# Sums of squares before a normalisation: six of eight tiles are added on VectorE, and TensorE multiplies ones with that sum and with the last two tiles

## The reference

```python
def rms_norm(x, gain):
    xf = x.astype(jnp.float32)
    y = xf * lax.rsqrt(jnp.mean(xf * xf, axis=-1, keepdims=True) + EPS)
    return (y * gain.astype(jnp.float32)).astype(x.dtype)

def swiglu(x, w_in, w_out):
    gate, up = jnp.split(x @ w_in, 2, axis=-1)
    return (jax.nn.silu(gate) * up) @ w_out

    for l in range(DEPTH):
        ...
        hn = rms_norm(h, g_ffn1[l]) * (1.0 + sc1) + sh1
        h = h + 0.5 * (1.0 + gt1) * swiglu(hn, w_ffn1_in[l], w_ffn1_out[l])
        hn = rms_norm(h, g_mix[l]) * (1.0 + sc2) + sh2
        proj = hn @ w_mix_in[l]
        ...
        h = h + (1.0 + gt2) * mixed
        hn = rms_norm(h, g_ffn2[l]) * (1.0 + sc3) + sh3
        h = h + 0.5 * (1.0 + gt3) * swiglu(hn, w_ffn2_in[l], w_ffn2_out[l])
```

## Time and profile before

| | |
|---|---|
| time, median of three runs | 3076.71 us (3075.94 to 3076.88) |
| span of the profiled execution | 3077.4 us |
| TensorE busy in it | 2896.3 us, 94% |
| VectorE busy | 1608.6 us, 52% |
| ScalarE busy | 980.8 us, 32% |
| GpSimd busy | 197.4 us, 6% |

### The profile page before, as it was taken

The page is one execution under the profiler, slowest core; times in us unless marked ns, Lnnn a source line. Parts: engine busy times, 40 slices in busy tenths (PEclk is TensorE's granted clock), DMA queues, the critical chain, the costliest instruction groups (busy, mean ns, idle before and its releaser), DMA issues.

```text
span 3077.4 us, 43060 instructions
## 1 busy us (share of the span) xinstructions
PE 2896.3 (94%) x17732; PEld 2329.1 (76%) x17732; DVE 1608.6 (52%) x2074; ACT 980.8 (32%) x1461; POOL 197.4 (6%) x270
## 2 busy tenths in 40 slices
PE   6999999988999998999999888999989999968996
PEld 5888877676788887888776767888767778658775
DVE  6676575763767524333357744333364446655533
ACT  2222223522322223222334323222324444422322
POOL 2000000230000000000001400000010000013000
PEclk8999999988999999999999889999999999969998
DMA  6556442102456322232211012232221121100231
GB/s 243 196 201 209 153 147 83 58 3 82 162 172 233 115 84 82 88 110 87 98 69 59 16 44 80 87 106 93 84 96 67 64 69 62 58 1 4 72 103 41
DMA packets 45368, 298.62 MB, mean 97 GB/s; under 512 B 5664, under 2 KB 5792, under 8 KB 16800
## 3 DMA queue, kind: packets, MB, share of 16 engines
q1 hardware_dynamic: 36000, 229.31, 22.0%
q0 software_dynamic: 9216, 67.11, 6.4%
HBM read 294.30 MB, written 2.10 MB: 96 GB/s over the span
## 4 chain that ended last, share of the span: by engine, by line
PE 86%; DVE 10%; ACT 2%; issue 1%; DMA 0%; POOL 0%; SPq 0%; DVEq 0%; ACTq 0%; POOLq 0%
PE ps L914 17%; PE ps L915 17%; PE ps L916 17%; PE ps L1181 5%; PE ps L1183 5%; PE ps L1182 5%; PE ps L821 1%; PE ps L1489 1%; PE ps L1490 1%; PE ps L1491 1%; PE ps L2019 1%; PE ps L2003 1%; PE ps L784 1%; PE ps L2016 1%; PE ps L1267 1%; DVE w_lo L891 1%
## 5 line engine op out<-in xcount | busy, mean ns | idle before, releaser
L914 PE MATMUL ps<-hn_hi,w_hi 128*128 128x512 f32 x1536 | 606.5, 395 | 33.9 <-DVE hn_lo L865 23.1
L915 PE MATMUL ps<-hn_lo,w_hi 128*128 128x512 f32 x1536 | 602.3, 392 | 0.0
L916 PE MATMUL ps<-hn_hi,w_lo 128*128 128x512 f32 x1536 | 601.4, 392 | 0.0
L891 DVE TENSOR_TENSOR w_lo<-w_raw,w_hi 128x2048 fp32r<-128x2048 f32 (+3 forms) x229 | 472.4, 2063 | 162.6 <-ACT w_hi L884 162.4
L884 ACT ACTIVATE w_hi<-w_raw 128x2048 fp32r<-128x2048 f32 (+3 forms) x229 | 394.4, 1722 | 115.6 <-PE ps L1183 98.0
L914 PEld LDWEIGHTS ps<-hn_hi,w_hi 128*128 128x128 f32 x1536 | 291.4, 190 | 100.4 <-issue 39.5
L1181 PE MATMUL ps<-hn_hi,w_hi 128*128 128x512 f32 x776 | 326.0, 420 | 20.4 <-DVE hn_lo L865 13.0
L915 PEld LDWEIGHTS ps<-hn_lo,w_hi 128*128 128x128 f32 x1536 | 291.2, 190 | 62.6 <-issue 2.0
L916 PEld LDWEIGHTS ps<-hn_hi,w_lo 128*128 128x128 f32 x1536 | 291.1, 190 | 60.9
L1183 PE MATMUL ps<-hn_hi,w_lo 128*128 128x512 f32 x776 | 306.7, 395 | 0.0
L1182 PE MATMUL ps<-hn_lo,w_hi 128*128 128x512 f32 x776 | 306.7, 395 | 0.0
(11 more groups left out here) (451 smaller groups left out, 3842.1 us busy)
## 6 DMA issues: line engine op xcount, KB each, us to landing
w_raw<-in_up SPq DMA_DIRECT2D x88, 1024.0 KB, 4.9
ada_w<-in_ada POOLq DMA_DIRECT2D x64, 1024.0 KB, 5.1
w_raw<-in_down SPq DMA_DIRECT2D x64, 704.0 KB, 4.1
w_raw<-in_mix_in SPq DMA_DIRECT2D x20, 1024.0 KB, 4.9
w_raw<-in_dsa_in SPq DMA_DIRECT2D x18, 1024.0 KB, 4.8
w_raw<-in_merge SPq DMA_DIRECT2D x16, 768.0 KB, 4.3
ada_first<-in_ada SPq DMA_DIRECT2D x8, 1024.0 KB, 17.1
w_raw<-in_mix_out SPq DMA_DIRECT2D x8, 1024.0 KB, 4.8
```

The costliest lines, as they stand in the source:

```text
L891: dve.tensor_tensor(w_lo[:, slot, 0:size], w_raw[:, slot, 0:size], w_hi[:, slot, 0:size].bitcast(F32), ALU.subtract).then_inc(w_lo_ready, 1)
L914: pe.matmul(bank, wh, x_hi[:, k], start=(k == 0), stop=False)
L915: pe.matmul(bank, wh, x_lo[:, k], start=False, stop=False)
L916: return pe.matmul(bank, wl, x_hi[:, k], start=False, stop=(k == K - 1))
```

## The change

The sum over tiles is split. VectorE adds the squares of tiles 0 to 5 elementwise into `rstd`, which is free at that time, in five instructions for each normalisation (`norm_add`, counted by a new semaphore `sq_added`). TensorE multiplies ones with that sum and then with the squares of tiles 6 and 7, all three after the stage's last piece (`norm_sums`). This holds for n = 1 to 7; n = 0 stays as it was. ScalarE's square j now waits for VectorE's add where it waited for TensorE's product, and `sq_summed` counts 2 for each later normalisation. On VectorE the second half of `down` is written out piece by piece where it was a loop. No transfer and no instruction of ScalarE is added or taken away.

```diff
--- before.py
+++ after.py
@@ -103,6 +103,7 @@
 S1, S2, O_BANK, E_BANK, LEVEL_BANK = 0, 1, 2, 3, 4
 PAIR_LOW, PAIR_UP, BEFORE, UP, LEVEL, EYE = 0, 1, 2, 3, 5, 10
 NEG = -1e30
+SQ_ADDS = 5
 VEC = {"mu": 8, "w0": 2, "a0": 2, "k_k": 2, "k_a": 2, "r_k": 2, "gn_w": 2, "gn_b": 2, "conv": 6, "q_gain": 1, "k_gain": 1}
 VEC_AT = {k: sum(list(VEC.values())[:i]) for i, k in enumerate(VEC)}
 NVEC = sum(VEC.values())
@@ -490,6 +491,7 @@
         act_f_ready = sem("act_f_ready")
         act_hi_ready = sem("act_hi_ready")
         sq_ready = sem("sq_ready")
+        sq_added = sem("sq_added")
         sq_summed = sem("sq_summed")
         norm_sqrt = sem("norm_sqrt")
         hn_tmp = sem("hn_tmp")
@@ -820,9 +822,28 @@
             pe.wait_ge(sq_ready, n * KD + j + 1)
             pe.matmul(small[1], ones[:], norm_squares(n)[:, j % 2], start=(j == 0), stop=(j == KD - 1)).then_inc(sq_summed, 1)
 
+        def norm_sums(pe, n):
+
+            pe.wait_ge(sq_added, SQ_ADDS * n)
+            pe.matmul(small[1], ones[:], rstd[:], start=True, stop=False)
+            for j in (KD - 2, KD - 1):
+                norm_sum(pe, n, j)
+
+        def norm_add(dve, n, j):
+
+            at = SQ_ADDS * (n - 1)
+            dve.wait_ge(sq_ready, n * KD + j + 1)
+            sq = norm_squares(n)
+            if j > 1:
+                dve.wait_ge(sq_added, at + j - 1)
+            dve.tensor_tensor(rstd[:], sq[:, 0] if j == 1 else rstd[:], sq[:, j % 2], ALU.add).then_inc(sq_added, 1)
+
         def norm_square(act, n, j):
             if j >= 2:
-                act.wait_ge(sq_summed, n * KD + j - 1)
+                if n:
+                    act.wait_ge(sq_added, SQ_ADDS * (n - 1) + max(1, j - 2))
+                else:
+                    act.wait_ge(sq_summed, j - 1)
             act.activation(norm_squares(n)[:, j % 2], h[:, j], ACT.Square).then_inc(sq_ready, 1)
 
         def norm_act(act, n, shift, last=False):
@@ -830,7 +851,7 @@
             if n == 0:
                 for j in range(KD):
                     norm_square(act, 0, j)
-            act.wait_ge(sq_summed, n * KD + KD)
+            act.wait_ge(sq_summed, KD + 2 * n)
             act.activation(rstd[:], small[1], ACT.Sqrt, bias=eps[:], scale=1.0 / D).then_inc(norm_sqrt, 1)
             if not last:
                 norm_act_out(act, n, shift)
@@ -958,9 +979,7 @@
                 else:
                     for i in range(KD):
                         down(i, i % 2)
-                        if i:
-                            norm_sum(pe, after_ffn(f), i - 1)
-                    norm_sum(pe, after_ffn(f), KD - 1)
+                    norm_sums(pe, after_ffn(f))
                 if (f, half, "down") in ada_batch:
                     pe_flush(pe, (f, half, "down"))
 
@@ -1052,11 +1071,17 @@
                     split_dve(dve, *ahead(p1, KD, TALL, i, odd))
                     if d_ada:
                         dve_ada(dve, d0 + i, (d0 + odd) % 2, d0 - later + i)
+                    if half and 2 <= i < SQ_ADDS + 2:
+                        norm_add(dve, after_ffn(f), i - 1)
                     dve.wait_ge(act_evac, p1 + i + 1)
                     hj = h[:, bass.ds(i, 1), :]
                     dve.scalar_tensor_tensor(hj, act_f[:, s:s + 1], out_gain[:, bass.ds(i, 1)], hj, ALU.mult,
                                              ALU.add).then_inc(dve_evac, 1)
-                steps(dve, KD, down)
+                if half:
+                    for i in range(KD):
+                        down(i, i % 2)
+                else:
+                    steps(dve, KD, down)
                 if (f, half, "down") in ada_batch:
                     a, b = ADA_FLUSH[f, half, "down"]
                     dve_flush(dve, own, ada_batch[f, half, "down"], ADA_FIRST + a, ADA_FIRST + b)
@@ -1508,11 +1533,7 @@
             nn = 3 * LAYERS + 1
             for i in range(4):
                 pe_piece(pe, p0 + i, (p0 + i) % 2, KD, 2, hn_hi, hn_lo, lambda k: None if i or k else pe.wait_ge(merged, 1))
-                if i:
-                    norm_sum(pe, nn, 2 * i - 2)
-                    norm_sum(pe, nn, 2 * i - 1)
-            norm_sum(pe, nn, KD - 2)
-            norm_sum(pe, nn, KD - 1)
+            norm_sums(pe, nn)
 
         def second_act(act):
             act.wait_ge(vec2_loaded, 16)
@@ -1829,12 +1850,17 @@
             def piece(i, odd):
                 s = (p0 + odd) % 2
                 split_dve(dve, *ahead(p0, 4, WIDE, i, odd))
+                if i > 1:
+                    norm_add(dve, 3 * LAYERS + 1, 2 * i - 2)
+                if i:
+                    norm_add(dve, 3 * LAYERS + 1, 2 * i - 1)
                 dve.wait_ge(act_evac, p0 + i + 1)
                 for t in range(2):
-                    hj = h[:, bass.ds(2 * i + t, 1), :].rearrange("p a t -> p (a t)")
+                    hj = h[:, 2 * i + t]
                     last = dve.tensor_tensor(hj, hj, tmp[:, s] if t == 0 else main[s][1], ALU.add)
                 last.then_inc(dve_evac, 1)
-            steps(dve, 4, piece)
+            for i in range(4):
+                piece(i, i % 2)
             dve.wait_ge(norm_sqrt, 3 * LAYERS + 2)
             own(dve.reciprocal(rstd[:], rstd[:]))
             for j in range(KD):
@@ -1916,14 +1942,9 @@
 
             def out_piece(i, odd):
                 pe_piece(pe, p1 + i, (p1 + odd) % 2, KD, 2, hn_hi, hn_lo, lambda k: None)
-            for i in range(1, KD // 2):
-                if i > 1:
-                    out_piece(i, i % 2)
-                if i:
-                    norm_sum(pe, 3 * l + 2, 2 * i - 2)
-                    norm_sum(pe, 3 * l + 2, 2 * i - 1)
-            norm_sum(pe, 3 * l + 2, KD - 2)
-            norm_sum(pe, 3 * l + 2, KD - 1)
+            for i in range(2, KD // 2):
+                out_piece(i, i % 2)
+            norm_sums(pe, 3 * l + 2)
 
         def mats_pe(pe, d, s):
 
@@ -2654,6 +2675,10 @@
                     split_dve(dve, (p1 + 2, p1 % 2), WIDE)
                 elif i != 1:
                     split_dve(dve, *ahead(p1, KD // 2, WIDE, i, odd))
+                if i > 1:
+                    norm_add(dve, 3 * l + 2, 2 * i - 2)
+                if i:
+                    norm_add(dve, 3 * l + 2, 2 * i - 1)
                 dve.wait_ge(act_evac, p1 + i + 1)
                 for t in range(2):
                     hj = h[:, bass.ds(2 * i + t, 1), :].rearrange("p a t -> p (a t)")
```

## The result

The changed kernel takes 3049.92 us (median of four executions, 3046.33 to 3051.88), the kernel before, timed beside it, 3076.8 us. The ratio is 0.9898 (95% interval 0.9879 to 0.9917): faster by some 27 us, 1.0%. The forecast was a gain of 35.8 us and a time of 3040.9 us; the median lies above the range of 3037.0 to 3045.5, and the gain is about three quarters of the forecast.

What follows compares the result with a forecast made beforehand. TensorE, busy for 94% of the span, was taken to bound the kernel. Savings of 21.2 + 3.5 + 3.5 + 7.6 = 35.8 us took 3076.7 to 3040.9 us, range 3037.0 to 3045.5.

Steps and rivals of the forecast that it cites:

- The price of a sum: Second halves of `down`, four stages: six sums between pieces cost 0.885 us each on TensorE; removing them saves 21.2 us.
- The pairs between pieces of `mix_out` and `last`: Pairs of sums cost 1.77 us each; removing those between pieces saves 3.5 us in `last`, 3.5 in two `mix_out` layers.
- The restart in `mix_out`: Third piece starts earlier without the pair behind the second: 3.8 us per layer, 7.6 in two; bounds 2.4 to 5.5 each.
- all terms of `mix_out` and `last` together: Savings forecast in these stages, from pairs between pieces and the earlier third piece of `mix_out`: 14.6 us.
- the third rival: Third piece of `mix_out` starts without gain because later weights come late: 7.6 us less gain, 3048.5 us; chance 0.03.
- part 5: Ends of `down`, `mix_out` and `last`: the changed products fit into TensorE's waits, so nothing is gained or lost.
- the second rival: Longer idle before the last two sums of `mix_out` and `last` drops the clock: 5.4 us in three stages, 3046.3; chance 0.05.
- VectorE as the pace in f = 0: Rival in `down`, f = 0: adds at 1.244 us make VectorE set the pace; 2.5 us less gain, 3043.4; chance 0.05.
- the last one, from the sum to the time and its range: Whole kernel: 35.8 us off 3076.7 gives 3040.9 us; own range 3037.5 to 3043.7 from restart bounds, stated range 3037.0 to 3045.5.

## Why the prediction was right and wrong

*The price of a sum, 0.885 us, 24 times (21.2 us): right.* All four second halves run at 7.48 us per piece; the run with `down` alone gained 24.6 us with a scatter of some 5 in single executions.

*The pairs between pieces of `mix_out` and `last` (7.0 us): right.* The third and fourth pieces of `mix_out` now end 10.9 us apart (ScalarE's copies at 745.15 and 756.04, 1820.88 and 1831.77), as do those of `last` (3015.28 and 3026.17).

*The restart in `mix_out` (2 x 3.8 us): right in the trace, 3.7 in each layer.* In the time it does not show: putting one pair back in each layer cost nothing where this term says 7.6 us, and all terms of `mix_out` and `last` together brought 4.7 us of 14.6. The time is near the third rival's 3048.5, to which I gave 0.03, but not by its mechanism: the third piece started early and its weights were not late. The stretches that ran faster without the changed restart are ones that no edit touches; why they did stays open. With small matmuls in both kernels the term has its size for that clock, 2.3 us in each layer.

*"Nothing here" for the ends of the stages (part 5): wrong.* This is the first step that failed. It is the second rival, to which I gave 0.05, at less than its price: I took 3.78 us for the two sums in three stages, 5.4 us in all, and they took 2.48 to 3.07 us in two stages, 1.5 to 2.0 us in all by the three traces of the changed kernel. I held it against this rival that the nearest row that had lengthened the work behind it had 2.87 us of idle time; at 1.94 us the clock fell in `mix_out` of both layers, not in `last`, where the idle time was 1.81. Filling that pause brought 6.3 us, more than the traces put there.

*The end of f = 0: 0.43 us that I had not counted.* The last update of h comes 0.43 us late (idle time of TensorE before the last sum 0.84 us behind one more sum, and the sum starts 2.96 us after the last matmul where it was 2.53). It is not the adds: with each doubled it stays the same. The last piece's `w_lo` is that of the next stage, 2.29 us in place of 1.63, behind a wait for ScalarE of 1.05 us; before, the longer period covered it. Part 5 had said that the last sum starts when it did.

*VectorE as the pace in f = 0: did not come*, not even with the adds doubled. (The row of 1.244 us that I took as the upper bound of an add is itself an add, not a product with a mask; no add came near it.) The Trainium skill's rule on the shared SBUF interfaces (GPSIMD Engine Reference, Key points) gave no lengthening here: the adds took 0.684 to 0.693 us, those in f = 0 beside GpSimd's issues among them.

*The second step that failed is the last one, from the sum to the time and its range.* It assumed that everything the change does not touch takes the same time again. The granted clock moved single stretches of it by 2 to 6.7 us, and single executions scatter with a standard deviation of 4.3 us (31 executions of before on four occasions, mean 3081.7). From that mean the same sum would have given 3045.9 us, so 5 us of the 9 between 3040.9 and the result are a start that was too low; the rest is missing in the gain. Three runs within 1 us of each other had hidden that. The range of 8.5 us held the sizes of the terms and no term for this. The Trainium skill's rule that I quoted (TensorE: Matmul & The Clock Gate, Part 1), that the slow stretch after a pause differs from run to run, I used for one restart alone. The traces agree with it elsewhere: behind the same 6.7 us of idle time the start of f = 1 ran at 0.50 for 3.6, 5.3 and 3.6 us in the three traces of the kernel before.

The gain of the changed kernel on the clock as it is: 28.2, 29.3 and 31.6 us in the means, on three occasions. With small matmuls in both kernels: 36.3 on one occasion, of which 3.9 lie in a stretch that the change does not touch. The 4 to 8 us between 28.2 to 31.6 and 35.8 are traced to the clock in part: 1.5 to 2.0 us at the ends of `mix_out`, and 0.43 us that are not the clock's at the end of f = 0. The rest goes with the granted clock in stretches that were not changed, and whether it is chance or comes from the change is open.

## What to carry to other kernels

Price an instruction that interrupts a stream by the distance between the pieces with and without it; its busy time is not that price. When work is taken off TensorE, look at what was filling its waits: a longer pause can give a part of the gain back at the lower clock (here 0.5 to 1.1 us for each sum taken out of such a place), and a few matmuls that nobody reads are a cheap way to hold the clock, here worth 14 us in 3050. The best version measured is the changed kernel with small matmuls in its pauses: 3032.86 and 3035.7 us, ratios 0.9828 and 0.9854 to the kernel before. Check a local saving in the time too: the saving at the restart of `mix_out` stood in every trace of the changed kernel and could not be found in the time. Before a forecast in tenths of a per cent, look at the low-clock stretches of the trace as a term of their own, since a second trace of the same kernel may have them elsewhere.

## What was not expected of the hardware

- An idle time of TensorE of 1.94 us was followed by a granted clock of 0.77 over the next 2.5 us in layer 0 and 0.64 over 3.1 us in layer 1. The same idle time was once not followed by a fall (layer 1 with the pair back: the sums took 1.98 us); idle times of 1.27 and 1.81 us were not in these traces.
- VectorE starts a new operation of 128x512 0.60 us after the last one, though each shows a duration of 0.68.
- Filling TensorE's waits with small matmuls brought 16.4 us in the kernel before and 13.7 us in the changed one, at a mean granted clock of 0.960 and 0.961 where it was 0.946 to 0.950.
